# Triangular inverses by doubling blocks: multiplying and copying only the block columns that a level keeps

## The reference, cut to what matters

```
kb = k * beta[..., None]
L = jnp.where(strict, jnp.einsum("bhnid,bhnjd->bhnij", kb, k) * decay, 0.0)
rhs = jnp.concatenate([v * beta[..., None], kb * jnp.exp(g)[..., None]], axis=-1)
sol = lax.linalg.triangular_solve(L, rhs, left_side=True, lower=True, ..., unit_diagonal=True)
```

```
sa = jnp.einsum('dbhij,dbhj->dbhi', state, a_t)
state = (state * w_t[..., None, :] + sa[..., :, None] * b_t[..., None, :]
         + v_t[..., :, None] * k_t[..., None, :])
y = jnp.einsum('dbhij,dbhj->dbhi', state, r_t)
```

## Time and profile before

| | us |
|---|---|
| median of 3 runs | 1714.46 (1705.96 to 1714.79) |
| the profiled execution, whole time | 1712.38 |
| its span on the core | 1710.2 |
| TensorE busy | 1592.5 (93%) |
| TensorE weight loads busy | 1528.2 (89%) |
| VectorE busy | 1055.4 (62%) |
| ScalarE busy | 728.0 (43%) |
| mean granted TensorE clock | 0.968 of full |

### The profile page before, as it was taken

One profiled execution on the slowest core, in us unless ns is written; L12 is line 12 of the kernel. 1 busy time (PEld: TensorE's weight loads), 2 busy tenths in 40 slices (PEclk: granted clock), 3 DMA queues, 4 the chain that ended last, 5 costly groups with the idle time before them and its releaser, 6 DMA issues.

```text
span 1710.2 us, 35864 instructions
## 1 busy us (share of the span) xinstructions
PE 1592.5 (93%) x15411; PEld 1528.2 (89%) x15411; DVE 1055.4 (62%) x1274; ACT 728.0 (43%) x811; POOL 67.4 (4%) x53
## 2 busy tenths in 40 slices
PE   7999999878899999999898999999969999899997
PEld 6999899777899999999888999999957778899997
DVE  4765577653666556764576665568666654776445
ACT  4443345532443344343455443464543322455333
POOL 1000000000100001000101000021110000100000
PEclk9999999989999999999899999999989998999999
DMA  8665545001566555655333665554200021455551
GB/s 280 199 196 177 189 131 169 26 2 39 172 195 194 188 173 177 193 196 192 128 100 124 197 196 181 189 175 140 74 2 2 2 101 51 159 181 177 189 190 41
DMA packets 155063, 243.23 MB, mean 142 GB/s; under 512 B 9283, under 2 KB 106174, under 8 KB 154814
## 3 DMA queue, kind: packets, MB, share of 16 engines
q1 hardware_dynamic: 154510, 240.63, 43.4%
q10 hardware_dynamic: 432, 0.79, 0.2%
HBM read 240.34 MB, written 1.05 MB: 141 GB/s over the span
## 4 chain that ended last, share of the span: by engine, by line
PE 81%; DVE 10%; ACT 5%; issue 2%; DMA 0%; POOL 0%; SPq 0%; DVEq 0%; ACTq 0%
PE dense_ps L2388 22%; PE dense_ps L2389 21%; PE dense_ps L2390 21%; PE mixer_ps L456 3%; DVE w_lo L2757 3%; ACT w_hi L2590 2%; PE dense_ps L456 2%; PE mixer_ps L1082 1%; PE mixer_ps L1655 1%; DVE qkv L887 1%; PE mixer_ps L1100 1%; PE mixer_ps L1091 1%; ACT ly_r L502 0%; PE mixer_ps L1661 0%; DVE h_lo L2824 0%
## 5 line engine op out<-in xcount | busy, mean ns | idle before, releaser
L2757 DVE TENSOR_TENSOR w_lo<-raw,w_hi 128x2048 fp32r<-128x2048 f32 x223 | 511.8, 2295 | 419.3 <-ACT w_hi L2590 418.5
L2388 PE MATMUL dense_ps<-h_hi,w_hi 128*128 128x256 f32 x2368 | 669.9, 283 | 29.0 <-DVE h_lo L2824 16.0
L2389 PE MATMUL dense_ps<-h_lo,w_hi 128*128 128x256 f32 x2368 | 662.2, 280 | 0.0
L2390 PE MATMUL dense_ps<-h_hi,w_lo 128*128 128x256 f32 x2368 | 661.9, 280 | 0.0
L2590 ACT ACTIVATE w_hi<-raw 128x2048 fp32r<-128x2048 f32 x223 | 427.7, 1918 | 505.1 <-PE dense_ps L2390 487.4
L2388 PEld LDWEIGHTS dense_ps<-h_hi,w_hi 128*128 128x128 f32 x2368 | 451.2, 191 | 37.4 <-issue 27.7
L2389 PEld LDWEIGHTS dense_ps<-h_lo,w_hi 128*128 128x128 f32 x2368 | 451.3, 191 | 0.8 <-issue 0.5
L2390 PEld LDWEIGHTS dense_ps<-h_hi,w_lo 128*128 128x128 f32 x2368 | 451.8, 191 | 0.0
L2388 PE MATMUL dense_ps<-g_hi,w_hi 128*128 128x256 f32 x960 | 267.4, 279 | 7.6 <-DVE full L2915 5.5
L2389 PE MATMUL dense_ps<-g_lo,w_hi 128*128 128x256 f32 x960 | 266.7, 278 | 0.0
L2390 PE MATMUL dense_ps<-g_hi,w_lo 128*128 128x256 f32 x960 | 266.7, 278 | 0.0
(11 more groups left out here) (526 smaller groups left out, 1845.9 us busy)
## 6 DMA issues: line engine op xcount, KB each, us to landing
raw<-in_ffn_w_gu SPq DMA_DIRECT2D x176, 512.0 KB, 4.7
raw<-in_ffn_w_down SPq DMA_DIRECT2D x88, 512.0 KB, 4.2
raw<-in_w_ff SPq DMA_DIRECT2D x64, 512.0 KB, 4.3
raw<-in_w_in SPq DMA_DIRECT2D x36, 512.0 KB, 4.4
raw<-in_a_w_in SPq DMA_DIRECT2D x32, 512.0 KB, 4.4
raw<-in_a_w_out SPq DMA_DIRECT2D x8, 512.0 KB, 4.3
raw<-in_b_w_in SPq DMA_DIRECT2D x8, 512.0 KB, 4.2
raw<-in_b_w_out SPq DMA_DIRECT2D x8, 512.0 KB, 4.2
```

What stands on the lines that cost most here:

```text
L2388: pe.matmul(o, hi, mh, start=start, stop=False)
L2389: pe.matmul(o, hi, ml, start=False, stop=False)
L2390: return pe.matmul(o, lo, mh, start=False, stop=stop)
L2757: dve.tensor_tensor(w_lo[:, p % 2, :], raw[:, p % RAW_SLOTS, :], w_hi[:, p % 2, :].bitcast(F32), ALU.subtract).then_inc(lo_ready, 1)
```

## The change

`quads` gets the level and a side. With `odd` 0 or 1 it addresses, in the operand that streams and in the result, only the even or the odd blocks of 2^lv columns: 32 columns of 64, in runs of 2^lv elements. The operand that is loaded as weights stays 64x64. The number of products stays, and so do all waits and their order. The Y products take the even side, except at level 1, where all 64 columns are kept so that the whole tile `y` is written once. ScalarE copies the even side alone at levels 2 to 5 (128x256 elements for 128x512), and the whole bank at levels 1 and 6. VectorE's work is unchanged.

```diff
-    def quads(pe, bank, half, lhs, rhs):
+    def quads(pe, bank, half, lhs, rhs, lv, odd):
+
+        def part(ap):
+            if odd is None:
+                return ap
+            return ap.rearrange("p (k e b) -> p k e b", e=2, b=1 << lv)[:, :, odd, :]
         for s4 in range(4):
             for q in range(2):
                 p_ = slice(64 * q, 64 * q + 64)
-                end_ = pe.matmul(bank[p_, P * s4 + 64 * q:P * s4 + 64 * q + 64], lhs(4 * half + s4)[p_, p_],
-                                 rhs(4 * half + s4)[p_, p_], start=True, stop=True)
+                end_ = pe.matmul(part(bank[p_, P * s4 + 64 * q:P * s4 + 64 * q + 64]), lhs(4 * half + s4)[p_, p_],
+                                 part(rhs(4 * half + s4)[p_, p_]), start=True, stop=True)
         return end_
...
-                    end_ = quads(pe, M_ps[:, half, :], half, nt_of, lambda s_: x[:, s_, :])
+                    end_ = quads(pe, M_ps[:, half, :], half, nt_of, lambda s_: x[:, s_, :],
+                                 lv, None if lv == 1 else 0)
...
-                    quads(pe, M_ps[:, half, :], half, lambda s_: xt[:, s_, :], lambda s_: y[:, s_, :])
-                    end_ = quads(pe, D_ps[:, half, :], half, lambda s_: y[:, s_, :], lambda s_: xt[:, s_, :])
+                    quads(pe, M_ps[:, half, :], half, lambda s_: xt[:, s_, :], lambda s_: y[:, s_, :], lv, 0)
+                    end_ = quads(pe, D_ps[:, half, :], half, lambda s_: y[:, s_, :], lambda s_: xt[:, s_, :], lv, 1)
...
-                act.activation(y[:, 4 * half:4 * half + 4, :], banks(half, 1), ACT.Copy).then_inc(y_kept, 1)
+                to, from_ = y[:, 4 * half:4 * half + 4, :], banks(half, 1)
+                if 1 < lv < LEVELS - 1:
+                    to, from_ = blocks(to, lv, 0), blocks(from_, lv, 0)
+                act.activation(to, from_, ACT.Copy).then_inc(y_kept, 1)
```

## The result

| | before | changed |
|---|---|---|
| median, us | 1710.73 (1705.96 to 1714.79, 4 runs) | 1726.49 (1724.01 to 1736.11, 4 runs) |
| ratio | | 1.0086, 95% interval 1.0051 to 1.0120 |
| span of the profiled execution, us | 1710.2 | 1724.4 |
| mean granted clock | 0.968 | 0.957 |

The kernel became slower by 0.9%, about 15 us. The prediction said slower; the time lies in its range, but the forecast of +41 us was more than two and a half times the measured loss.

A forecast was written before the change was run, and what follows sets the result against it. TensorE, busy for 93% of the span, was taken as the bound. Products at no change, low clock +43 us, half of the copies' 3.8 us saved: net +41 on 1712.4, forecast 1754 us, range 1703 to 1785.

The forecast's parts named there:

- The products: Matrix products inside the inverses on TensorE: halving the streamed columns was costed at no change of pace.
- the load alone holds the pace: TensorE pieces in the inverses: a 64-column weight load, 0.055 of 0.058 us per pair, sets the pace whatever streams.
- the last piece of a burst was to land sooner: Hand-overs from TensorE to the next engine: some 27 ns sooner, about 60 on the path, 1.6 us at most.
- the clock term: TensorE in the six batches: streaming less drops the granted clock to half, costing 43 us; chance 0.62.
- The copies: ScalarE's narrowed copies at levels 2 to 5: 0.21 us less for each of 18 that TensorE waits for, 3.8 us.
- The price of a batch that is low for 85%: RWKV batches: 9.0 us for low clock throughout, 7.7 us with the first level at full clock, 31 us in four.
- the same case: Changed batches read as like the last level at 1287.0 to 1290.4, about half the pieces, then clock 0.50.
- the sums between the levels: Other products between RWKV levels: two groups of about 0.6 us doubled at low clock, some 1.3 us a batch.
- the clock be low for half the time: Two delta-rule batches: 9 us for half the time at low clock plus 3 us for 512-column products, 12 us.
- the first rival: Granted clock holds in the batches, so only copies and hand-overs count: 4.8 us less, 1707.6 us; chance 0.23.
- That the stream sets the pace: TensorE pieces speed up with half the stream: 28 us gained after VectorE's limits, 1684 us; chance 0.07.
- that short runs cost something: Levels 0 and 1: runs of one and two elements slow TensorE, 17 us less 4 us, 1725 us; chance 0.08.

The follow-up runs named there:

- e6_stream_32_in_one_run: Changed kernel with the 32 streamed columns in one run instead of blocks, merge masks zero, output not the reference's; ratio 1.0113 (1.0027 to 1.0199).

## Why the prediction was right or wrong

**The products: right in the sum.** "I cost the narrower stream at no change of pace" holds at clock 1.00 (0.46 us), at 0.50 (0.85 us), and down to 16 columns. The estimate that the load alone holds the pace was half the truth: the stream needs nearly as long (0.44 to 0.45 us with half the load). The earlier trace rows could not tell them apart, since at 128 and 128 columns both take 0.10 to 0.11 us. The next two loads of the group at 307.62, whose pieces stream 512 columns, could have told:

```profile
308.16 0.19 PEld L571 LDWEIGHTS mixer_ps<-g_upto,cst 128*128 128x128 f32 x1 [0.24 <-issue]
308.59 0.19 PEld L571 LDWEIGHTS mixer_ps<-g_upto,cst 128*128 128x128 f32 x1 [0.24 <-issue]
```

They are 0.43 us apart, four times 0.11 us: there the stream sets the pace. The 27 ns by which the last piece of a burst was to land sooner are there (321 and 294 ns), and the 0.2 to 0.3 us a batch of the narrow products fit the 1.6 us put down for them. (Half of 58 ns is 29, not 27; and the upper bound of the clock term, 70 + 15 us, gives 1797 us, over the 1785 us at which the range ends.)

**The copies: right.** 0.21 us each, forecast 3.8 us, 4.8 us measured for them alone (1.0 to 8.6 us by its interval); the six batches of the two traces differ by 169.6 - 165.4 = 4.2 us.

**The clock: right in kind, its share wrong, its price somewhat low.** The step that failed is the share of time at the low clock. The price of a batch that is low for 85% was put at 7.7 us. The batches with a stream of 16 were low for 73% of their time on average and cost 32.4 - 23.7 = 8.7 us each; that this kernel's loss of 49 us is close to the sum that I had made for the changed kernel is thus in part luck. For each us at low clock the RWKV batches lost 0.35 us in the changed kernel (9.6 us in 27 us, against narrow copies alone) and 0.37 us with a stream of 16 (34.7 us in 94 us), where the forecast comes to 9.0 / (23.7 + 9.0) = 0.28. It let the longer bursts cover 4.0 us of waits a batch; how much of that failed was not measured.

The share came from one reading. I wrote that the changed batches are "the same case" as the last level at 1287 to 1290.4, and "with a first level still at full clock I take 85%". In the trace the RWKV batches were low for 17.0 us, 0, 10.3 us and 0: 27 of 104.5 us, 26%. I had also written that a low clock would have no reason to rise "until long products come", and had counted the sums between the levels, +1.3 us a batch, as a cost only. Both rises came right behind the longest of them, six pieces of 256 columns (lines 1563 and 1615, from 1291.3 and from 1377.1). That they are what lifts the clock is not shown: in `e6_stream_32_in_one_run` the same pieces pass, and the clock stays low.

The RWKV batches lost 5.5 + 3.6 us and gained 1.1 + 1.0 us, in all +7.0 us where the forecast had +31 before the copies. In the delta rule I let the clock be low for half the time, and it was (0.78 and 0.80 are 44% and 40%), but before it was low for 28% and 10% already (0.86 and 0.95), which I had not subtracted: +4.8 us in place of +12.

So the comparison with the last level was too harsh. It had half the pieces, waits of 0.3 to 0.5 us between them, and a longer one at its end, from 1290.0:

```profile
1291.10 2.05 PE L1661 MATMUL mixer_ps<-v_tok_r,gram_raw 128*128 128x128 f32 x8 [1.10 <-DVE xt_raw L521]
```

The clock fell at 1290.4, inside this wait, and not "with loads still going", as the first rival was answered. The changed batches have narrow pieces with waits of this size mainly in their first two levels. This fits what was seen, that some batches kept the clock, that it fell early in those that did not, and that products alone, with longer waits, cost 33 to 37 us where the changed kernel cost 15 to 23 in its two measurements (about 5 us of the difference is what the copies save by themselves). These two kernels are the only pair with narrow products that differs in the waits, and which batches fall differs between them in other ways too, so it stays an argument. The forecast had this case too: the lower end of its own range, 1725 us, was the clock "low in a third of it". It took the other end as the likely one.

**The rivals.** That the clock holds was true of two RWKV batches of four. That the stream sets the pace, and that short runs cost something, are refuted by streams of 16 and of 32 in one run.

**Still open:** why it is just the first and the third RWKV batch, in two executions, when other edits make other batches fall; and whether narrowing only the later levels would keep the clock. The choice is not a fixed property of these batches, since the first two fell with X Y alone narrow and only the first with one run of 32.

## What to carry to other kernels

Before trimming a product, read which of weight load and stream sets its pace; if they are equally long, only cutting both pays much. On a TensorE-bound stretch, work that is taken out of the stream without shortening the time can cost more than it saves: here the granted clock fell in batches that streamed less, above all where TensorE also waited. Watch the clock of the stretch, not only the busy time. When two cases of the trace bracket the changed kernel, price both ends and say that it may lie anywhere between, rather than taking it for the nearer one; and before calling two stretches the same case, compare their waits.

## What the runs showed of the hardware

- 64x64 float32 pieces in two quarters side by side: 0.46 us for 16 with 64 load columns, whether 16, 32 or 64 columns stream; 0.44 to 0.45 us with 32 load columns and 64 streamed; 0.25 us with 32 and 32. At clock 0.50, with 64 load columns: 0.85 us.
- The granted clock fell in 4 of 4 RWKV batches with 16 streamed columns, in 2 of 4 with 32 in blocks (3 of 4 with whole copies) and 1 of 4 with 32 in one run, in none with 64, at the same number of pieces and the same pace at clock 1.00, so weight loads did not by themselves keep it up. These are counts of one profiled execution each (two for the changed kernel). With the same 32 columns at nearly twice the pace it mostly held (0.92 to 1.00).
- In the changed kernel the clock fell in the first 5.6 us of a batch and rose again within it, after 17.0 and 10.3 us, while the narrow pieces went on. A low stretch can last longer with less to stream: the one that came with the first delta-rule batch lasted 6.8 us before and with narrow copies alone, and 13.7 us in both traces of the changed kernel. With the Y products alone narrow it lasted 10.2 us, with the others alone 6.8 us.
- The result of a burst is there 27 ns sooner with 32 streamed columns than with 64 (ScalarE starts 294 and 321 ns after the last load), and 40 ns sooner with 16 (281 ns).
- With 32 in place of 64 contraction rows at one level and the same columns, the clock went from 1.00 to 0.95 in three RWKV batches and to 0.98 in the fourth, in one profiled execution; the mean clocks of all twelve executions lean the same way (0.964 to 0.971, against 0.969 to 0.975).
- Runs of 1 to 32 elements in the streamed operand and in the result cost TensorE nothing (32 pieces of level 0, in runs of one, take 1.12 us from 1364.02, and 1.15 us with all 64 columns before), and ScalarE's copy in runs of 4 to 32 takes 384 ns like the plain one, while VectorE's masked copy with runs of 1 takes 0.74 us instead of 0.44 us.
